# Attention in a transformer layer: the position bias of near key tiles is added by VectorE instead of by two identity products on TensorE

## The reference

```python
# mixer A: each position attends to its 256 best keys (chosen by an indexer); 8 heads, one key/value head
logits = jnp.einsum('bqhd,bqkd->bhqk', qb, kg) * scale
bias = bias_a[t5_bucket(q_pos[None, :, None] - sel)]     # one number per head and bucket of distance
logits = jnp.where(valid[:, None], logits + transposed(bias), -jnp.inf)
p = jax.nn.softmax(logits, axis=-1)
# mixer B: sliding window of 128, 8 query heads on 2 key heads, a learned sink per head
logits = jnp.where(mask, logits + bias_b[t5_bucket(dist)], -jnp.inf)
p = exp(logits - m) / (sum(exp(logits - m)) + exp(sink - m))
```

## Time and profile before

| what | value |
|---|---|
| median of 3 runs | 3627.24 us (3626.94 to 3629.5) |
| the profiled execution, whole | 3625.67 us |
| its span, first to last instruction | 3623.6 us |
| stage of attention | about 780 to 1612 us |
| TensorE busy in the span | 3391.3 us, 94% |
| VectorE busy in the span | 2506.4 us, 69% |
| granted TensorE clock, mean | 0.977 of full speed |

### The profile page before, as it was taken

The page is one execution under the profiler, slowest core; times in us unless marked ns, Lnnn a source line. Parts: engine busy times, 40 slices in busy tenths (PEclk is TensorE's granted clock), DMA queues, the critical chain, the costliest instruction groups (busy, mean ns, idle before and its releaser), DMA issues.

```text
span 3623.6 us, 40448 instructions
## 1 busy us (share of the span) xinstructions
PE 3391.3 (94%) x15020; PEld 2697.7 (74%) x15064; DVE 2506.4 (69%) x4097; ACT 1661.5 (46%) x2030; POOL 677.7 (19%) x370
## 2 busy tenths in 40 slices
PE   7999999968888999969899999999999999999997
PEld 5788778855556666647777888888888888888886
DVE  5899999987776766536555765567566766576566
ACT  5767888126566666663222333333333333333332
POOL 1012132334455656650000000000000000000001
PEclk9999999979999999989999999999999999999998
DMA  6322233352211120027554432223332332223230
GB/s 168 50 90 94 93 105 103 117 158 72 52 51 40 43 59 24 17 66 213 174 163 117 151 128 93 92 83 128 122 105 93 108 128 92 97 102 112 92 105 32
DMA packets 232927, 356.36 MB, mean 98 GB/s; under 512 B 43421, under 2 KB 150573, under 8 KB 218782
## 3 DMA queue, kind: packets, MB, share of 16 engines
q1 hardware_dynamic: 231678, 349.42, 31.2%
q0 software_dynamic: 1056, 4.36, 0.3%
HBM read 289.60 MB, written 64.13 MB: 98 GB/s over the span
## 4 chain that ended last, share of the span: by engine, by line
PE 50%; DVE 2%; ACT 1%; DMA 1%; issue 1%; POOL 0%; SPq 0%; DVEq 0%
PE tl_ps L88 17%; PE tl_ps L89 17%; PE tl_ps L90 17%; DMA tl_pr<-in_w_pb_dram 0%; DVE tl_stat L1449 0%; PE tl_ps L1643 0%; DVE tl_sg L1439 0%; ACT tl_ph L1330 0%; DMA tl_yr<-yt 0%; DVE tl_xr L1459 0%; DVE tl_xr L1466 0%; DVE tl_nmr L1538 0%; ACT tl_woh L1350 0%; ACT tl_sg L1332 0%; DVE tl_xr L1467 0%
## 5 line engine op out<-in xcount | busy, mean ns | idle before, releaser
L90 PE MATMUL tl_ps<-tl_xh,tl_ul 128*128 128x512 f32 x1536 | 597.5, 389 | 0.0
L88 PE MATMUL tl_ps<-tl_xh,tl_uh 128*128 128x512 f32 x1536 | 597.5, 389 | 0.0
L89 PE MATMUL tl_ps<-tl_xl,tl_uh 128*128 128x512 f32 x1536 | 597.5, 389 | 0.0
L1378 ACT ACTIVATE tl_c<-tl_ps,tl_cb,tl_cw 128x512 f32<-128x512 f32 x192 | 148.8, 777 | 748.5 <-PE tl_ps L90 748.5
L789 POOL TENSOR_TENSOR plo<-pf,phi 128x1024 fp32r<-128x1024 f32 x168 | 415.7, 2476 | 345.1 <-ACT phi L838 344.9
L88 PE MATMUL frt_acc<-frt_xh,frt_wh 128*128 128x512 f32 x864 | 339.2, 393 | 18.7 <-issue 8.7
L89 PE MATMUL frt_acc<-frt_xl,frt_wh 128*128 128x512 f32 x864 | 338.1, 391 | 0.0
L90 PE MATMUL frt_acc<-frt_xh,frt_wl 128*128 128x512 f32 x864 | 337.8, 391 | 0.0
L88 PEld LDWEIGHTS tl_ps<-tl_xh,tl_uh 128*128 128x128 f32 x1536 | 288.3, 188 | 60.0
L90 PEld LDWEIGHTS tl_ps<-tl_xh,tl_ul 128*128 128x128 f32 x1536 | 288.3, 188 | 59.9
L89 PEld LDWEIGHTS tl_ps<-tl_xl,tl_uh 128*128 128x128 f32 x1536 | 288.3, 188 | 59.6
(11 more groups left out here) (270 smaller groups left out, 7460.1 us busy)
## 6 DMA issues: line engine op xcount, KB each, us to landing
tl_ur<-in_w_up_dram SPq DMA_DIRECT2D x96, 1024.0 KB, 4.8
tl_dr<-in_w_down_dram SPq DMA_DIRECT2D x64, 768.0 KB, 4.4
zt<-frt_out SPq DMA_DIRECT2D x108, 256.0 KB, 4.6
frt_wr<-in_w_main_dram SPq DMA_DIRECT2D x51, 512.0 KB, 4.2
att_raw<-zt SPq DMA_DIRECT2D x64, 256.0 KB, 4.1
tl_sg<-zt SPq DMA_DIRECT2D x64, 256.0 KB, 4.5
frt_xr<-in_xt_dram SPq DMA_DIRECT2D x12, 1024.0 KB, 7.5
yt<-y SPq DMA_DIRECT2D x32, 256.0 KB, 2.3
```

Source lines behind the costliest of these rows:

```text
L88: pe.matmul(out, ahi, bhi, start=first, stop=False)
L89: pe.matmul(out, ahi, blo, start=False, stop=False)
L90: return pe.matmul(out, alo, bhi, start=False, stop=last)
L1378: act.activation(c[:, k % 2, a, :], up(k, a), ACT.Identity, scale=cw[:, 2, a, k % NS:k % NS + 1], bias=cb[:, a, k % NS:k % NS + 1]).then_i ...
```

## The change

The two identity products of each half of each near step go, and with them `blo`, its making on VectorE (`low_near`) and the identity `idr`. ScalarE's copy of the bias stays, in float32. VectorE gets a part in the entry `logits`: in a near step it reads the logits from PSUM, adds the bias in float32 and writes the sum to `pf` in SBUF. ScalarE's exponential of a near step then waits for VectorE's `bs`, not for TensorE's `std`, and reads and writes `pf`. The buffer `stp` of a near step is free when VectorE has read it. A far step stays as it was. The order of `plan` is not changed.

```diff
+        def near_of(b, i):
+            kind, n = seq[b]
+            return (1 - i if kind else n - i) if kind or n - i < 2 else None
+        sums = [sum(near_of(*u) is not None for u in steps[:k]) for k in range(len(steps) + 1)]
...
-        bhi = s.sb("bhi", [P, 2, 2, QW], F32R)
-        blo = s.sb("blo", [P, 2, 2, QW], F32R)
+        bias = s.sb("bias", [P, 2, 2, QW], F32)
...
-                act.activation(bhi[:, kind], near[:, kind], ACT.Copy).then_inc(S["bhd"], 1)
+                act.activation(bias[:, kind], near[:, kind], ACT.Copy).then_inc(S["bhd"], 1)
...
             def exponential(k):
-                act.wait_ge(S["std"], k + 1)
-                if k == 0:
-                    act.wait_ge(S["bld"], 2)
-                    act.wait_ge(S["rnd"], 3)
-                if k >= PS:
-                    act.wait_ge(S["pv"], k - PS + 1)
-                act.activation(pf[:, k % PS, :], stp[:, k % 2, :], ACT.Exp).then_inc(S["ex"], 1)
+                if near_of(*steps[k]) is not None:
+                    act.wait_ge(S["bs"], sums[k + 1])
+                    src = pf[:, k % PS, :]
+                else:
+                    act.wait_ge(S["std"], k + 1)
+                    if k >= PS:
+                        act.wait_ge(S["pv"], k - PS + 1)
+                    src = stp[:, k % 2, :]
+                act.activation(pf[:, k % PS, :], src, ACT.Exp).then_inc(S["ex"], 1)
                 act.wait_ge(S["ex"], k + 1)
                 act.activation(phi[:, k % PS, :], pf[:, k % PS, :], ACT.Copy).then_inc(S["ph"], 1)
...
-            def low_near(kind):
-                dve.wait_ge(S["bhd"], kind + 1)
-                dve.tensor_tensor(blo[:, kind], near[:, kind], f32(bhi[:, kind]), ALU.subtract).then_inc(S["bld"], 1)
+            def add_bias(b, i):
+                kind, n = seq[b]
+                k, near = first[b] + i, near_of(b, i)
+                if near is None:
+                    return
+                dve.wait_ge(S["bhd"], 2)
+                dve.wait_ge(S["rnd"], 3)
+                dve.wait_ge(S["std"], k + 1)
+                if k >= PS:
+                    dve.wait_ge(S["pv"], k - PS + 1)
+                dve.tensor_tensor(pf[:, k % PS, :], stp[:, k % 2, :], bias[:, kind, near, :], ALU.add).then_inc(S["bs"], 1)
...
-            dve.tensor_copy(idr[:], ident[:]).then_inc(S["cst"], 1)
...
                     if b == 0:
-                        low_near(0)
                         low_values()
-                    elif b == 1:
-                        low_near(1)
...
+                elif op == "logits":
+                    add_bias(b, x)
                 elif op == "top":
                     top(b, x)
...
-                if k >= 2:
+                if k >= 2 and near_of(*steps[k - 2]) is not None:
+                    pe.wait_ge(S["bs"], sums[k - 1])
+                elif k >= 2:
                     pe.wait_ge(S["ex"], k - 1)
...
-                    if near is not None:
-                        pe.matmul(o, idr[:], bhi[:, kind, near, cols], start=False, stop=False)
-                        last = pe.matmul(o, idr[:], blo[:, kind, near, cols], start=False, stop=True)
```

## The result

The changed kernel takes 3717.07 us (median of 4 runs, 3712.31 to 3723.82) against 3628.37 us before (median of 4, 3626.94 to 3631.32): ratio 1.0243, 95% interval 1.0226 to 1.0261, so 89 us slower. The forecast was 58 us, the range ended at 3712. So shifts read from the two traces add up to 98 us and not to 89.

The account below looks back on a forecast made before the run. The early stretch was taken as bound by a VectorE-ScalarE-TensorE chain, the late mostly by TensorE. Early +54.5, late +7.8, start -4.6 gave +57.7 us on 3625.67, 3683.4; with the median 1.6 above, 3685 us, range 3640 to 3712.

Parts of the forecast that it names:

- What bounds the kernel: Attention stage: early, a chain over VectorE, TensorE and ScalarE through `vt` sets the pace; late (from 1160 us), mostly TensorE.
- The removed products: Near steps: 252 products at 0.226 us go, 57 us of TensorE, or 0.91 us a near step.
- The start of the stage: Before the first tops: two VectorE instructions of 2.29 us go from the path, 4.6 us gained whole.
- The price of an addition: VectorE, near steps: 63 additions at 1.22 us, upper bound 1.63, so 77 to 102 us of VectorE.
- The early near steps: Cycles 0 to 7: exponentials queue behind VectorE and delay the chain, shifts of +4.8 to +9.5 us, together +54.5.
- the delay stays: Early cycles, after L980: VectorE is the bound again, so the delay (+5.8 us in cycle 6) persists.
- rival D: Early stretch: more idling lowers the granted clock, 14 us at most on top; C with it 0.10.
- the late list: Cycles 8 to 15: shifts from +4.1 us in cycle 9 to -2.2 each in 14 and 15, together +7.8.
- A: Whole stage: TensorE is the bound throughout, so -45 us, 3582 us; chance 0.06.
- B: Chain shorter than walked, early additions cost only their own 37.8 us: +12.7, 3640 us; 0.15 including up to the forecast.
- C: VectorE sets the pace in every near step, or additions stretch: +72 to +98, 3700 to 3725 us; 0.10 with D.
- E: Near steps: the bias is not added where the profile can show it (no VectorE group of 63); no chance given.

Follow-up runs that it names:

- order_only: Kernel before with all its products, plus an 8-column VectorE copy per near step for which that step's exponential waits: 3693.19 us, ratio 1.0183.
- no_products: Kernel before without its 252 identity products and nothing in their place (bias of near steps left out): 3617.02 us, ratio 0.9974.
- nop8: Kernel before without the identity products in cycles 8 to 15 alone, the early ones kept: 3598.75 us, ratio 0.9919.
- fill: Changed kernel plus zero-weight TensorE products before `vt` in 11 of the 14 waits: 3704.8 us, ratio 1.0217.
- late8: Changed kernel with additions in cycles 8 to 15 only, products kept in cycles 0 to 7: 3650.46 us, ratio 1.0064.
- keep: Changed kernel with four zero-weight products in each near step in place of the four removed: 3743.36 us, ratio 1.0324.
- load_only: Kernel before plus a 128x1024 VectorE reduction from SBUF at each near step, for which nobody waits: 3646.3 us, ratio 1.0055.

## Why the prediction was wrong, point by point

- **What bounds the kernel**: right. Early it is the chain over VectorE and ScalarE, which order_only shows by lengthening it with next to no work.
- **The removed products**, 57 us of TensorE: right in size, and right that they are no gain early. Still too kind: without an addition their removal costs 14 to 22 us there (no_products against nop8). Late, 3.7 us a cycle as worked out.
- **The start of the stage**: right. The first queries' low part to the first top was 9.0 us before and is 4.6 now:

```profile
801.39 1.22 DVE L979 SCALAR_TENSOR_TENSOR att_qst<-att_raw,att_qst 64x1024 fp32r<-64x1024 f32 x1 [5.90 <-issue]
...
806.02 0.28 DVE L946 CUSTOM_DVE_ANT_0 att_junk<-att_sq,att_cm 128x128 bf16<-128x128 f32 x1
```

- **The price of an addition**: right, 1224 ns.
- **The early near steps**: right in the sum. Counted from TensorE's first near logits, which takes in the first addition as the walk did, cycle 6 was forecast +5.8 us up to L980 and measured +6.4, cycle 7 +6.0 and +6.4, cycle 5 +9.5 and +7.6. In cycle 1 it was +8.0 and +12.9: the first near logits start at 849.31, but VectorE comes to their addition only at 854.91, behind an eviction and reciprocals, and their exponential is 4.8 us later than before. Cycles 0 to 7 came to 58.7 us against 54.5 foreseen.
- **The step that failed first**: "the delay stays", that is, between L980 and the next near steps the kernel only shifts. These stretches grew by 20.1 us before cycles 1 to 8, of which 16.2 lie before cycles 1 to 7. I had the cause as rival D, "if the early stretch fell to 0.9 ... 14 us, would be the most". It fell to 0.80. I had priced the clock from the two means that the trace before showed, 0.95 and 0.99, though my own walk made TensorE's idle times of 1 us before `vt` into such of 7 and 8 us. fill shows that the clock rises and the stretches shrink when these are filled: it gave back 13.2 of the 20.1 us and reached five of the seven early waits before `vt`, none of them whole. What the other waits cost was not measured apart.
- **The step that failed second**: the late list, +7.8, which measured +24.1 behind cycle 7 in the trace (and 20 to 24 in late8). I had walked the chain up to the next top and left out who else stands behind a late exponential on ScalarE: the eviction of the mixer before, for which TensorE's first values of the next entry wait. In cycle 10, step 87's exponential starts at 1375.38 behind VectorE's addition, the evictions end at 1383.0, and TensorE waits 3.62 us. TensorE's waits for these evictions rose by 8.1 us over the whole stage, so they are at most half of the 16.3 us that were missing. The clock after 1160 us fell to 0.92 as well, which the list had not counted; how the rest divides is open.

```profile
1375.38 1.06 ACT L842 ACTIVATE pf<-pf 128x1024 f32<-128x1024 f32 x1 [2.95 <-DVE pf L903]
...
1382.62 0.38 ACT L854 ACTIVATE y<-att_ov 64x256 f32<-64x256 f32 x1
```

```profile
1383.14 0.47 PE L1111 MATMUL att_ov<-phi,att_vhb 128*128 128x512 f32 x1 [3.62 <-ACT y L854]
```

- **The sum, term by term**, in the trace: start of the stage -4.4 us (forecast -4.6), early near steps +58.7 (+54.5), stretches behind them up to cycle 7 +16.2 (nothing), late cycles +24.1 (+7.8), outside the stage +3.5 (nothing): 98 us against 58.
- **Rivals**: A is refuted (keep shows that the saved products are worth 28 us and not 57, and the changed kernel is slower). B, in which idle time of VectorE takes the queueing up, is refuted by order_only. C, additions at VectorE's pace everywhere, named 3700 to 3725 us and the result lies in it, but for another reason: load_only costs 21 us and not 72. E is refuted by the group of 63.
- **The rule of the Trainium skill** (Perfetto Trace Analysis, Identifying the Most-Contended Engine): weight loads as the measure of TensorE pointed the right way in the early stretch. In the late one it gives 290 us against VectorE's 265, and the change still lost 20 to 24 us there: an occupancy does not see an order.

## What to carry to other kernels

Moving work to an engine with idle time is not free when another engine's short operations queue behind its result: ask what stands behind the new wait on the waiting engine, not only how long the new operation is. Two changes of order gave back 66 of 89 us here. And an operation of TensorE that runs beside a bound elsewhere may be worth keeping: take it away only in the stages that TensorE bounds.

## What the runs showed of the hardware that I had not expected

- The granted clock fell strongly where TensorE idled more: 0.95 (before), 0.88 (products removed), 0.86 (fill), 0.80 (changed) from 817 to 1160 us of the same stage. After a wait of 8.35 us products came every 0.42 us.
- Products of zero weights raised it too (0.80 to 0.86 with fill), so that a kernel with more work for TensorE was the faster one, by 9 us.
- An addition of 128x1024 with an operand in PSUM stayed between 1161 and 1225 ns in all 63 cases, while L979, with both operands in SBUF, took 1222 to 1990 ns in 32.
